# The last unit of each head pair in a hybrid attention kernel: second head's keys, values, then first head's keys

## What is computed

```python
def mla_expand(ckv, w_kv_up, k_nope_norm):
    B, S, _ = ckv.shape
    kv = (ckv @ w_kv_up).reshape(B, S, MLA_HEADS, QK_NOPE + V_HEAD)
    return rmsnorm(kv[..., :QK_NOPE], k_nope_norm), kv[..., QK_NOPE:]

def mla_attend(q_nope, q_pe, k_nope, k_pe, v, mask):
    s = (jnp.einsum('bqhd,bshd->bhqs', q_nope, k_nope)
         + jnp.einsum('bqhd,bsd->bhqs', q_pe, k_pe)).astype(jnp.float32) * ATTN_SCALE
    ...
    p = jax.nn.softmax(s, axis=-1).astype(v.dtype)
    return jnp.einsum('bhqs,bshd->bqhd', p, v)
```

## Time and profile before

| what | value |
|---|---|
| median of 3 runs | 1999.95 us (1999.67 to 2000.25) |
| the profiled execution, its own time | 1999.66 us |
| its span in the profile | 1997.9 us |
| PE busy | 1988.2 us (100% of the span), weight loads 98% |
| DVE, ACT, POOL busy | 61%, 46%, 10% |
| granted clock of PE | at its full value in all 40 slices |
| the eight pairs | from about 228 to 520 us of the span |

### The profile page before, as it was taken

One profiled execution on the slowest core, in us unless ns is written; L12 is line 12 of the kernel. 1 busy time (PEld: TensorE's weight loads), 2 busy tenths in 40 slices (PEclk: granted clock), 3 DMA queues, 4 the chain that ended last, 5 costly groups with the idle time before them and its releaser, 6 DMA issues.

```text
span 1997.9 us, 36175 instructions
## 1 busy us (share of the span) xinstructions
PE 1988.2 (100%) x14810; PEld 1963.9 (98%) x14810; DVE 1211.7 (61%) x2330; ACT 909.5 (46%) x1810; POOL 192.3 (10%) x228
## 2 busy tenths in 40 slices
PE   9999999999999999999999999999999999999998
PEld 9999999999999999999999999999999999999998
DVE  7856677676576576666765555444455665555554
ACT  5564455565444443434444444444444543333333
POOL 0011143434200000000000001000000000000000
PEclk9999999999999999999999999999999999999999
DMA  9765434343464554645545655555656566666665
GB/s 250 202 187 150 116 117 119 97 117 112 127 175 137 158 159 128 179 127 173 157 139 170 170 169 166 169 170 169 174 169 170 170 184 193 193 193 193 193 193 142
DMA packets 219262, 323.24 MB, mean 162 GB/s; under 512 B 28240, under 2 KB 100264, under 8 KB 219096
## 3 DMA queue, kind: packets, MB, share of 16 engines
q1 hardware_dynamic: 215800, 317.71, 55.3%
q10 hardware_dynamic: 3296, 3.22, 0.5%
HBM read 310.06 MB, written 9.62 MB: 160 GB/s over the span
## 4 chain that ended last, share of the span: by engine, by line
PE 98%; SPq 1%; DMA 0%; DVE 0%; ACT 0%; issue 0%; ACTq 0%
PE bank L1847 30%; PE bank L1851 30%; PE bank L1850 30%; PE bank L2113 1%; PE bank L2083 1%; PE bank L2009 1%; PE bank L2012 1%; PE bank L2011 1%; PE bank L2185 0%; PE bank L2211 0%; PE bank L2079 0%; SPq L469 0%; PE bank L2080 0%; DMA raw<-in_w_in_dram 0%; DMA xt<-in_meta_tokens_dram 0%; PE bank L2238 0%
## 5 line engine op out<-in xcount | busy, mean ns | idle before, releaser
L1205 DVE TENSOR_TENSOR wlo<-raw,whi 128x512 fp32r<-128x512 f32 (+1 forms) x1256 | 812.9, 657 | 731.5 <-ACT whi L796 723.7
L1847 PE MATMUL bank<-xsplit,whi 128*128 128x288 f32 (+2 forms) x4128 | 1217.0, 295 | 3.7 <-DVE xsplit L1229 2.7
L1851 PE MATMUL bank<-xsplit,wlo 128*128 128x288 f32 (+2 forms) x4128 | 1211.5, 293 | 0.0
L1850 PE MATMUL bank<-xsplit,whi 128*128 128x288 f32 (+2 forms) x4128 | 1211.2, 293 | 0.0
L796 ACT CAST whi<-raw 128x512 fp32r<-128x512 f32 (+1 forms) x1256 | 706.7, 576 | 957.7 <-PE bank L1851 915.3
L1847 PEld LDWEIGHTS bank<-xsplit,whi 128*128 128x128 f32 (+1 forms) x4128 | 772.6, 187 | 6.9 <-issue 5.1
L1850 PEld LDWEIGHTS bank<-xsplit,whi 128*128 128x128 f32 (+1 forms) x4128 | 772.6, 187 | 1.9 <-issue 1.0
L1851 PEld LDWEIGHTS bank<-xsplit,wlo 128*128 128x128 f32 (+1 forms) x4128 | 772.1, 187 | 0.0
L1847 PE MATMUL bank<-latents,whi 128*128 128x288 f32 (+1 forms) x352 | 112.7, 320 | 0.1
L1850 PE MATMUL bank<-latents,whi 128*128 128x288 f32 (+1 forms) x352 | 106.9, 304 | 0.0
L1851 PE MATMUL bank<-latents,wlo 128*128 128x288 f32 (+1 forms) x352 | 106.7, 303 | 0.0
(11 more groups left out here) (303 smaller groups left out, 1229.5 us busy)
## 6 DMA issues: line engine op xcount, KB each, us to landing
raw<-in_w_in_dram SPq DMA_DIRECT2D x313, 512.0 KB, 3.8
raw<-in_w_out_dram SPq DMA_DIRECT2D x128, 512.0 KB, 3.9
raw<-in_w_in_dram SPq DMA_DIRECT2D x142, 256.0 KB, 3.1
raw<-in_w_q_up_dram SPq DMA_DIRECT2D x48, 384.0 KB, 3.3
raw<-in_w_kv_up_dram SPq DMA_DIRECT2D x16, 512.0 KB, 3.6
xres<-in_x_prompt_dram SPq DMA_DIRECT2D x32, 128.0 KB, 3.9
xt<-in_x_prompt_dram SPq DMA_DIRECT2D x28, 128.0 KB, 5.1
out_dram<-ytok SPq DMA_DIRECT2D x28, 128.0 KB, 3.5
```

Of the source, the lines that this page charges most:

```text
L1205: ins = tt(lo, src, hi.bitcast(f32), ALU.subtract)
L1847: ins = mm(out, w_hi, m_hi, start=start, stop=False, **kw)
L1850: mm(out, w_hi, m_lo, start=False, stop=False, **kw)
L1851: return mm(out, w_lo, m_hi, start=False, stop=stop, **kw)
```

## The change

In the last of the four key and value units of every pair the order is now: second head's keys (bank 0), values (banks 1 and 2), first head's keys (bank 3). The other three units stay as they were. The helpers take the two heads in the same order, second before first (`K_ORDER = (1, 0)`), and DVE copies bank 0, bank 1, bank 3. In the group behind the last pair, the first unit takes the banks 0, 1, 2, 3 instead of 0, 1, 3, 2. No instruction is added or removed.

```diff
+K_ORDER = (1, 0)
...
-                k_square_hi(phase, i, n, 0)
-                k_square_hi(phase, i, n, 1)
+                for t in K_ORDER:
+                    k_square_hi(phase, i, n, t)
...
             def k_square_lo(n):
 
-                for t in range(2):
-                    dve.wait_ge(k_sq, 2 * n + t + 1)
-                    dve.wait_ge(k_sqh, 2 * n + t + 1)
+                for nth, t in enumerate(K_ORDER):
+                    dve.wait_ge(k_sq, 2 * n + nth + 1)
+                    dve.wait_ge(k_sqh, 2 * n + nth + 1)
                     tt(ksl[:, t, :], sq2[:, t, :], ksh[t].bitcast(f32), ALU.subtract).then_inc(k_sql, 1)
...
             def pair_end(i, n):
-                for t in range(2):
-                    k_evict("step", i, n, t)
+                k_evict("step", i, n, K_ORDER[0])
                 v_evict("step", i, n)
+                k_evict("step", i, n, K_ORDER[1])
                 k_square_lo(n)
...
-                    for h, b in ((0, 3), (1, 0)):
+                    def key_rows(h):
+
+                        b = (3, 0)[h]
...
+                    if last:
+                        key_rows(1)
+                    else:
+                        key_rows(0)
+                        key_rows(1)
...
+                    if last:
+                        key_rows(0)
...
             def k_squares(phase, i, j):
-                for t in range(2):
+                for nth, t in enumerate(K_ORDER):
                     b = 6 + t
-                    pe.wait_ge(k_sql, 2 * j + t + 1)
+                    pe.wait_ge(k_sql, 2 * j + nth + 1)
...
-            group(U_ML, "ml0v", 0, 0, 0, attention("ml0v", 0, 7), turn=(0, 1, 3, 2))
+            group(U_ML, "ml0v", 0, 0, 0, attention("ml0v", 0, 7), turn=(0, 1, 2, 3))
...
             def k_square(phase, i, n):
-                for t, b in ((0, 3), (1, 0)):
+                for t in K_ORDER:
+                    b = (3, 0)[t]
```

More of the change, by code:

```diff
@@ L1435, in _ @@
             steps(PAIR_UNITS, pair_units(0), pair_units(1), first_pair)
-            for t in range(2):
-                k_evict("bulk0", 0, 0, t)
+            k_evict("bulk0", 0, 0, K_ORDER[0])
             dve.wait_ge(ck_tail_out, 32)
             v_evict("bulk0", 0, 0)
+            k_evict("bulk0", 0, 0, K_ORDER[1])
             k_square_lo(0)
@@ L1996, in kv_units @@
                             ins.then_inc(full[b], 1)
+                        return ins
+                    if last:
[3 more added lines that the diff above has]
+                        key_rows(1)
                     def vcols(w):
```

## The result

The changed kernel took 2005.57 us (median of 8 runs, 2004.77 to 2006.33), the kernel before 1999.81 us beside it (8 runs, 1999.37 to 2001.66): ratio 1.0027, 95% interval 1.0018 to 1.0036. It is slower, by 5.8 us; the forecast was 2004.9. The span of the profiled execution is 2003.2 us, 5.3 more than before's 1997.9.

A forecast was written before the change was run, and what follows sets the result against it. PE, busy throughout, was taken to wait for POOL's norms at the transposes, behind `q_scale`. Six pairs at 0.82 (4.9), first +0.1, last 0: +5.0 on 1999.66 gives 2004.7 profiled, 2004.9 us median; range 2001.0 to 2006.0.

The forecast's parts named there:

- The chain without slack: From `q_scale` to PE's transposes, 10.55 us: any delay of `q_scale` delays PE in full, in the first seven pairs.
- the 0.08: At the transposes' weight load: PE is held 0.08 us now (0.21 less 0.13), the most a faster chain gives back.
- Bank 2: Next pair's first matmul into bank 2: its 0.16 us wait for ACT's copy goes away, useful only if the chain allows.
- PE's work is the same: First step, at a pair's end: PE's work stays unchanged, while bank 2 is full 0.58 us earlier.
- rival 2: POOL's square and DVE's subtraction run side by side: not slower, 1.8 us gained, 1998.1 us; chance 0.12.
- Turns between DVE and POOL: Between pair end and `q_scale`: two-input DVE and POOL instructions run one at a time; POOL's square makes `q_scale` 0.84 later.
- my play: Second pair's helper instructions stepped through with undisturbed lengths: `q_scale` ends at 302.66 instead of 301.82, 0.84 us later.
- my rule of 0.14: DVE and POOL on SBUF: the waiting instruction begins 0.14 us before the other's recorded end; who asked first goes first.
- Rival 4: Every DVE and POOL hand-over waits for the other's recorded end: 0.28 us more per pair, 2006.6 us; chance 0.04.
- First pair: At its end DVE's first subtraction goes ahead of POOL's square, `q_scale` 0 to 0.3 later: +0.1 us.
- Last pair: At its end POOL is 3.4 us early at the transposes and the units are longer: 0 us added.
- Rival 3: DVE's subtraction gets in ahead of POOL's square in all pairs: 0.1 to 0.5 per pair, 2000.5 to 2003; chance 0.15.

The follow-up runs named there:

- delay_scale: The kernel before, with one useless DVE instruction of 0.67 us directly ahead of `q_scale`: 2003.70 us, ratio 1.0018.
- delay_late: The kernel before, with the same useless DVE instruction behind `q_norm` in unit 14, where nobody waits for it: 1999.74 us, ratio 0.9997.
- copies_act_before: The kernel before, with POOL's four rounded query copies made by ACT ahead of `k_rstd`, POOL's wait for `q_turn`'s end left in: 1999.71 us, ratio 0.9995.
- short_square: The changed kernel, but POOL squares only 16 of the first head's 432 key columns, the rest set to 1 in idle time: 2001.99 us, ratio 1.0007.
- copies_act_after2: The changed kernel with POOL's four rounded copies on ACT and without POOL's leftover wait for `q_turn`'s end: 1999.07 us, ratio 0.9993.
- turn_between: As copies_act_after2, but POOL makes `q_turn` between its two squares: 1998.73 us, ratio 0.9992 against the kernel before.
- copies_act_after: The changed kernel with POOL's four rounded copies on ACT, POOL's wait for `q_turn`'s end left in: 2004.72 us, ratio 1.0022.

## Why the prediction was right

**The chain without slack.** Right, and shown by itself: delay_scale made 0.59 us of PE out of 0.59 on DVE, delay_late nothing. The other half of the sentence, that a faster chain gives back no more than 0.08 a pair, holds as a bound, but the 0.08 itself was misread: PE was not held there. Only the load was 0.08 late; the matmul behind it starts 17.84 after the first key copy with the late load and with the early one (copies_act_before).

**Bank 2.** The 0.16 us at the matmul into bank 2 went away, as forecast, and nothing of it is in the time, since PE only came earlier to the wait for POOL. But "PE's work is the same" was wrong by 0.08 us a pair, the longer last unit. That is why the next pair's first matmul comes at 296.69 - 294.85 = 1.84 after the first key copy instead of 1.77, and `q_scale` ends 6.24 after that matmul and not 6.3. The price of rival 2, in which PE would have got back 0.16 + 0.08 a pair, was too high for both reasons: 0.08 a pair is what the two kernels show in which PE waits for nobody.

**Turns between DVE and POOL.** Right in mechanism and nearly in size. Counted from the first key copy, my play put `q_scale`'s end at 8.08 (302.66 - 294.58), and the trace has 8.08. That it fits to 0.01 is partly luck: the steps before ran 0.06 to 0.07 later than played, since bank 3 was full later by the longer unit (the second subtraction ended at 5.24 instead of 5.18, the fourth rest at 7.00 instead of 6.93), and the first scaling got in some 0.05 earlier than my rule of 0.14 lets it. The square met the subtraction, which became 1.17 long; rival 2, in which they run side by side, would have had 0.61. Rival 4 would have given 0.28 more a pair. The one choice that was off is that I took 0.82 as the middle of what close races could give, where the play said 0.84: 6 x 0.84 = 5.0 instead of 4.9. That the square, and not the late bank 3 alone, is most of the cause is shown by short_square, which took away 0.57 of the 0.84.

**First pair.** The order was right, subtraction before square, and the term too small: +0.27 instead of +0.1. For `q_scale` the play gave 0 to 0.3 later; counted from the first key copy the trace has 7.38 instead of 7.05, +0.33, just over it.

**Last pair.** 0, as forecast, in the time: the span from its first key copy to the end is the same before and after. POOL is early at the transposes there as I said. The sum is 5.3 instead of 5.0, which is what the profiled executions show (2005.00 against 1999.66). The medians are 5.8 apart, because the changed kernel's profiled execution lies 0.57 under its median and before's only 0.15.

**Rival 3**, a subtraction ahead of the square in all pairs, came in the first pair alone.

Open: the fifth pair is 0.28 longer up to its transposes than its neighbours (18.06 against 17.79), before and after the change alike (18.90 against 18.63), so it is no part of the result. The trace of before puts it on ACT: the first exponential starts 0.37 after the end of the maximum before it (L1454), where in the fourth pair it is 0.10. copies_act_before and copies_act_after2 don't have it; its cause was not found. Nor is it settled that turn_between is faster than before: 1.4 us is less than a measurement of this kernel tells.

## What to carry to other kernels

When an order on the busiest engine is changed to free a resource sooner, look for the next place where that engine waits: a wait removed ahead of another wait is worth nothing, and whatever the new order adds to the chain behind the second wait is paid in full. Price the helpers by playing their instructions through with undisturbed lengths, above all where DVE and POOL newly meet on SBUF. Check also that the reordered engine's own work keeps its length: here it grew by 0.08 us a pair, half of what the order saved. And shorten the chain that has become late: POOL's copies moved to ACT took back the whole loss (1.1 us under the kernel before instead of 5.8 over it).

## What I had not expected of the hardware

A share of busy time of 98% (weight loads) and 100% (matmuls) stood over all these kernels, whether PE waited or not. The spacing of the loads pointed to the places, but it is no measure of what they cost. The load at the transposes came 0.21 behind the one before it instead of 0.13 in the kernel before, and no matmul was late by it; in the changed kernel it came 0.33 behind, and the middle pairs were some 0.84 longer. What counts is when the matmul starts, counted from a fixed point of the same pair.

A wait that is already satisfied is not free on POOL: with it the norms began 0.12 to 0.13 us after the reciprocals (copies_act_after and copies_act_before), without it 0.05 (copies_act_after2). Through the turns with DVE these 0.07 us became 0.84 us of norms (3.52 against 2.68) in each of the six middle pairs of copies_act_after, and 5.4 us of the kernel (4.3 over before against 1.1 under); in copies_act_before they became at most 0.14 and cost nothing. I had expected 1998.3 to 1999.3 us of copies_act_after since I played through only the part up to `q_scale` and took the rest of the chain as rigid: its length holds only as long as POOL's instructions meet DVE's in the same phase.
